# Tile 1's front moved from before the gathers to beside the first 66 slots, and projection passes over tiles 0-1, 2-5, 6-8

## The reference

```python
xn = rms_norm(x, attn_norm)
proj = xn @ w_in                         # 1024 -> 3328: q, k (rotated), v, and 1792 columns for time mixing
o_da = rms_norm(attend(q, k, v, lam), da_subln) * (1.0 - lam_init)      # two softmax maps per head, 4 heads
o_rw = rwkv_time_mix(p_rw, ...)          # recurrent state, 8 heads of 64
h = x + concat([o_da, o_rw]) @ w_out
h = h + peer_ffn(rms_norm(h, ffn_norm), peer_wq, peer_sub_keys, peer_u, peer_v)
```

```python
q = (xb @ wq).reshape(PEER_CHUNK, PEER_HEADS, 2, PEER_KD)
s = jnp.einsum('thcd,hcnd->thcn', q, sub_keys)
sv, si = lax.top_k(s, PEER_TOPK)
cand = (sv[:, :, 0, :, None] + sv[:, :, 1, None, :]).reshape(PEER_CHUNK, PEER_HEADS, -1)
bv, bi = lax.top_k(cand, PEER_TOPK)
act = jax.nn.gelu(jnp.einsum('thkd,td->thk', u_tab[eidx], xb))
return jnp.einsum('thk,thkd->td', gate * act, v_tab[eidx])
```

## Time and profile before

| what | value |
|---|---|
| time, median of 3 runs | 3935.95 us (3930.47 to 3946.15) |
| the profiled execution | 3929.9 us |
| its span, first to last instruction | 3928.1 us |
| busy: PE, DVE, ACT, POOL | 73%, 66%, 33%, 35% of the span |
| moved by DMA | 1431.66 MB, mean 364 GB/s |
| first and last gather issued | 745.5 us, 3895.4 us |

### The profile page before, as it was taken

The page is one execution under the profiler, slowest core; times in us unless marked ns, Lnnn a source line. Parts: engine busy times, 40 slices in busy tenths (PEclk is TensorE's granted clock), DMA queues, the critical chain, the costliest instruction groups (busy, mean ns, idle before and its releaser), DMA issues.

```text
span 3928.1 us, 54696 instructions
## 1 busy us (share of the span) xinstructions
PE 2876.3 (73%) x20366; PEld 1348.2 (34%) x20366; DVE 2599.3 (66%) x5836; ACT 1289.5 (33%) x3597; POOL 1367.6 (35%) x1190
## 2 busy tenths in 40 slices
PE   6899999775678676766766776677576758866565
PEld 3654454342224232322332243224232315521111
DVE  2422456398568948884987598768866776446954
ACT  1311211334332524342434334433433224432232
POOL 1000000244334434443444343434343456533453
PEclk9999999887787787878777777878777667777565
DMA  8534524799999999999999999999999999999998
GB/s 312 196 142 172 194 73 166 307 420 420 422 419 402 420 422 410 419 409 420 413 418 402 419 412 411 385 419 412 393 410 393 375 343 414 405 408 422 416 408 355
DMA packets 254827, 1431.66 MB, mean 364 GB/s; under 512 B 27521, under 2 KB 45457, under 8 KB 110305
## 3 DMA queue, kind: packets, MB, share of 16 engines
q0 software_dynamic: 163232, 1162.26, 72.6%
q1 hardware_dynamic: 91328, 265.89, 17.9%
HBM read 1373.21 MB, written 54.85 MB: 364 GB/s over the span
## 4 chain that ended last, share of the span: by engine, by line
DMA 25%; DVE 17%; PE 16%; issue 5%; POOL 1%; ACT 1%; another core or an unknown queue 0%; SPq 0%; DVEq 0%; ACTq 0%; POOLq 0%
DMA pe_buf<-in_experts,pe_idx 24%; DVE pe_buf L2312 6%; PE pe_psO L1466 4%; PE pe_psH L1448 2%; PE pe_B L1412 2%; POOL pe_buf L1040 1%; PE pe_B L1365 1%; DVE pe_few L2082 1%; PE pe_B L1111 1%; PE pe_B L1304 1%; DMA op_w<-in_w_out 1%; PE pe_B L1395 1%; DVE pe_topi L2191 0%; PE pe_B L1118 0%; PE pe_psW L1436 0%
## 5 line engine op out<-in xcount | busy, mean ns | idle before, releaser
L1040 POOL DMA_INDIRECT pe_buf<-in_experts,pe_idx x1088 | 1281.2, 1178 | 2442.9 <-PE pe_psO L1466 1637.1
L2312 DVE CUSTOM_DVE_ANT_0 pe_buf<-pe_buf,pe_hnR 128x1024 f32<-128x1024 f32 x1088 | 1316.5, 1223 | 695.0 <-DMA pe_buf<-in_experts,pe_idx 647.4
L1466 PE MATMUL pe_psO<-pe_buf,pe_Z 128*32 128x256 f32 x8704 | 843.8, 485 | 631.6 <-ACT pe_Z L1744 599.4
L1738 ACT ACTIVATE pe_gelu<-pe_dot 128x1 f32<-128x1 f32 x1088 | 219.2, 201 | 1622.7 <-DVE pe_dot L2312 1570.2
L1466 PEld LDWEIGHTS pe_psO<-pe_buf,pe_Z 128*32 128x32 f32 x8704 | 215.2, 123 | 1299.0 <-ACT pe_Z L1744 993.5
L1448 PE MATMUL pe_psH<-pe_hn,pe_pick 128*128 128x512 f32 x544 | 415.8, 856 | 44.9 <-ACT pe_hnR L1720 41.3
L1077 PE MATMUL ip_B<-ip_w,ip_xT 128*128 128x512 f32 (+1 forms) x1008 | 430.4, 577 | 16.2 <-DMA ip_w<-in_w_in 16.2
L1744 ACT ACTIVATE pe_Z<-pe_gl,pe_gelu 128x8 f32<-128x8 f32 x1088 | 327.2, 301 | 43.3 <-PE pe_psO L1466 0.4
L1412 PE MATMUL pe_B<-op_wkr,pe_mix 128*128 128x512 f32 (+1 forms) x576 | 270.0, 613 | 9.5 <-DMA op_wkr<-scratch_wk_rows 9.4
L1077 PEld LDWEIGHTS ip_B<-ip_w,ip_xT 128*128 128x128 f32 x1008 | 190.0, 194 | 211.1 <-issue 205.6
L1448 PEld LDWEIGHTS pe_psH<-pe_hn,pe_pick 128*128 128x128 f32 x544 | 108.9, 247 | 175.6 <-issue 88.8
(11 more groups left out here) (344 smaller groups left out, 3600.6 us busy)
## 6 DMA issues: line engine op xcount, KB each, us to landing
op_wkr<-scratch_wk_rows SPq DMA_DIRECT2D x36, 2048.0 KB
ip_w<-in_w_in SPq DMA_DIRECT2D x18, 2048.0 KB, 9.0
op_w<-in_w_out SPq DMA_DIRECT2D x9, 2560.0 KB
pe_buf<-in_experts,pe_idx POOLq DMA_INDIRECT x1088
op_w<-in_w_out SPq DMA_DIRECT2D x9, 1024.0 KB
ip_w<-in_peer_wq SPq DMA_DIRECT2D x4, 2048.0 KB, 11.2
scratch_wk_rows<-wk_wkc SPq DMA_DIRECT2D x16, 512.0 KB, 6.0
tm_ps<-scratch_moved_rows SPq DMA_DIRECT2D x8, 896.0 KB
```

What stands on the lines that cost most here:

```text
L1040: pool.indirect_dma_start(buf[b][:], None, T["experts"], bass.IndirectOffsetOnAxis(ap=idx[:, t % 2, h * NJ + j:h * NJ + j + 1], axis=0)).t ...
L1466: last = nc.tensor.matmul(psO[32 * x:32 * x + 32, j // 4, :], Z[:, n % NZ, 24 - 8 * turn:56 - 8 * turn], buf[home[n]][:, D + x * QUART:D + ...
L1738: nc.scalar.activation(gelu[:, col:col + 1], dot[:, col:col + 1], ACT.Gelu_apprx_tanh).then_inc(f["gelu_done"], 1)
L2312: nc.vector.tensor_tensor_reduce(buf[b][:, 0:D], buf[b][:, 0:D], hnR[:, n // PH % 2, :], 1.0, 0.0, ALU.mult, ALU.add, dot[:, n % (NBUF + E ...
```

## The change

Four things change together.

1. The passes of the projection go over tiles 0-1, 2-5 and 6-8 in place of tile 0, tiles 1-4 and tiles 5-8. The turns move accordingly: four turns stand ahead of the first unit, and four in a row behind the last unit of pass 0. x of tile 1 is loaded ahead of the second block of `w_in`.
2. The front of tile 1 leaves the third phase of the fill, but for its first 20 steps. The other 119 are dealt over slots 0 to 65.
3. The later fronts are dealt with a lag: the front of tile 2 ends at slot 40 of tile 1, that of tile 3 at slot 36 of tile 2, and so on to slot 20 of tile 6 for tile 7. The front of tile 8 ends where it did, at slot 64 of tile 7.
4. `topk` of tile t + 1 can start only when that tile's front has been dealt, so it starts at slot 68 in tile 0 and at slots 42, 38, 34, 30, 26 and 22 in tiles 1 to 6, in place of slot 2. It ends at slot 120 as before.

```diff
-PASSES = ((0,), (1, 2, 3, 4), (5, 6, 7, 8))
+PASSES = ((0, 1), (2, 3, 4, 5), (6, 7, 8))
+N0 = NG * len(PASSES[0])
...
-    steps = [("turn", 0, 0), ("turn", 0, 1)]
+    steps = [("turn", t, half) for t in PASSES[0] for half in range(2)]
...
+NEXT_IN_FILL = 20
...
-        ((("ip", (IP_HALF, IP_STEPS)),), (("tm", 1), ("at", 1), ("op", 1)), (("topk", 0),)))
-DURING = tuple((("tm", t + 2), ("at", t + 2), ("op", t + 2)) for t in range(LAST - 1))
+        ((("ip", (IP_HALF, IP_STEPS)),), (("next", (0, NEXT_IN_FILL)),), (("topk", 0),)))
+NEXT = (("tm", 1), ("at", 1), ("op", 1))
+DURING = ((("next", (NEXT_IN_FILL, None)),),)
+DURING += tuple((("tm", t + 2), ("at", t + 2), ("op", t + 2)) for t in range(LAST - 1))
...
-TOPK_FROM, TOPK_FROM_LAST, TOPK_TO = 2, 66, 120
+LATE = (40, 36, 32, 28, 24, 20) + (LAST_OP_BY,)
+FRONT_BY = (66,) + tuple((t + 1) * 128 + late for t, late in enumerate(LATE))
+TOPK_FROM = (68,) + tuple(late + 2 for late in LATE)
+TOPK_TO = 120
...
-        length = PER if t < len(DURING) - 1 else PER + LAST_OP_BY
+        length = FRONT_BY[t] - len(plan)
...
                         load_w(0)
+                        load_x(1)
+                        load_rope(0)
                         load_w(1)
-                        load_rope(0)
-                        load_x(1)
```

More of the change, by code:

```diff
@@ L12 @@
+import itertools
 from contextlib import ExitStack
@@ L151 @@
 NU = NG * NT
-PASSES = ((0,), (1, 2, 3, 4), (5, 6, 7, 8))
+PASSES = ((0, 1), (2, 3, 4, 5), (6, 7, 8))
+N0 = NG * len(PASSES[0])
 UNITS = tuple((t, n) for tiles in PASSES for n in range(NG) for t in tiles)
 def turns_after(g):
[L159 to L164, removed]
+    after = {(0, 1): [(2, 0)], (1, 1): [(2, 1)], (0, 3): [(3, 0)], (1, 3): [(3, 1)],
+             (1, NG - 1): [(4, 0), (4, 1), (5, 0), (5, 1)], (2, NG - 1): [(6, 0)], (3, NG - 1): [(6, 1), (7, 0)],
+             (4, NG - 1): [(7, 1)], (6, 0): [(8, 0), (8, 1)]}
+    return after.get(UNITS[g], [])
 def fold_order():
@@ L232, in steps_of @@
         return arg[1] - arg[0]
+    if stage == "next":
+        return sum(steps_of(i) for i in NEXT) - arg[0] if arg[1] is None else arg[1] - arg[0]
     if stage == "at":
@@ L244, in costs_of @@
             costs += [ip_cost(i) for i in range(*item[1])]
+        elif item[0] == "next":
+            costs += costs_of(NEXT)[item[1][0]:item[1][1]]
         else:
@@ L324, in topk_pulls @@
     def topk_pulls(t, k):
-        first = TOPK_FROM if t < LAST - 1 else TOPK_FROM_LAST
+        first = TOPK_FROM[t]
         n = TOPK_TO - first
@@ L334, in through @@
             for kind, arg in items:
-                yield from range(arg) if kind == "gap" else stage[kind](arg)
+                if kind == "next":
+                    yield from itertools.islice(following, steps_of((kind, arg)))
+                else:
+                    yield from range(arg) if kind == "gap" else stage[kind](arg)
+        following = through(NEXT)
         for streams in FILL:
@@ L365, in bank_of @@
     def bank_of(g):
-        return (g if g < NG else g + len(FOLD)) % 3
+        return (g if g < N0 else g + len(FOLD)) % 3
     def evicted(eng, units):
@@ L378, in fold_bank @@
     def fold_bank(u):
-        return (NG + u) % 3
+        return (N0 + u) % 3
     def fold_evicted(u):
@@ L1063, in project @@
                             pe.wait_ge(ip["xT"], 2 * t + 2)
-                            if NG <= g < NG + 3:
-                                half, n_ = fold_evicted(len(FOLD) + g - NG - 3)
+                            if N0 <= g < N0 + 3:
+                                half, n_ = fold_evicted(len(FOLD) + g - N0 - 3)
                                 pe.wait_ge(wk_out[half], n_)
@@ L1088, in fold_keys @@
                 if u < 3:
[L1089 removed]
+                    pe.wait_ge(ip["copied"], copied_of(N0 + u - 2))
                 else:
```

2 lines of the change are left out of this document (1 added, 1 removed).

## The result

The changed kernel takes **3981.97 us** (3981.05 to 3984.26, four runs) against 3934.14 us (3930.47 to 3946.15, four runs) for the kernel before: ratio **1.0127**, 95% interval 1.0112 to 1.0141. The forecast was 3928 us, no change to be told, in a range from 3880 to 3982 us. It is slower, by about 48 us, and stands at the upper end of that range. The main part grew by more than 110 us, which the prediction named as a sign that it is wrong. The profiled execution has a span of 3982.5 us, 54.4 more than before.

What follows compares the result with a forecast made beforehand. PE was taken to bound the fill and DMA the main part, with DVE close behind. Terms -92 + 40 + 15 + 15 + 8 + 6 = -8 gave 3928 us on the median, range 3880 to 3982.

Steps and rivals of the forecast that it cites:

- the fill: Before the first gather: PE work and waits leave with tile 1's front; -92 us, from -78 to -105.
- moved transfers: Main part: 16.8 MB of loads moved out of the PE-bound start onto DMA at 420 GB/s; +40 us.
- first 66 slots: Tile 0, slots 0 to 65: 119 front steps packed densely, engine chain may hold up slots; +15 us, 0 to +50.
- tile 2's front: Squeezed into 71 slots from slot 66 on, DVE needing 209 us against DMA's 192; +8 us, 0 to +17.
- `topk` beside `tm` and `at`, tiles 3 to 7: 78 us more DVE work against 79 us of gather waits, nearly balancing; +15 us, 0 to +78.
- tile 8's front: It has 172 slots in place of 192 and part of `topk` beside it; +6 us, 0 to +20.
- the second rival: Slots 42 to about 130 of each tile: DVE becomes the bound beside `tm` and `at`; +64, 4000 us; 21%.
- Its test: Slots 42 to 130 of tiles 1 to 5: DMA share 0.95 or less would prove DVE the bound.
- DVE needed ... 209: 71 slots from slot 66: 215 us before, less 23 for 19 dots, plus 17 of `topk`, makes 209 us.
- the fourth rival: First 66 slots: PE at half clock makes them 253 us against 205, +48 not +15; 3961 us; 3%.
- the third: Start before gathers doesn't shrink as it should; its third phase keeps some 30 us; +22, 3958 us; 4%.
- The first: Main part: slots absorb moved `topk` and tile 1's front at DMA's pace; -52, 3884 us; 35%.

Runs made afterwards that it cites:

- the kernels without it: Kernel before and changed kernel, each with DVE's choice of experts left out for tiles 1 to 8: 3900.59 us and 3853.61 us.
- the lag alone: Kernel before with the changed kernel's dealing of the fronts of tiles 2 to 8 and of `topk`; 4009.19 us, ratio 1.0206.
- `topk` over slots 8 to 91: Kernel before with `topk` of tiles 1 to 7 dealt over slots 8 to 91, not 2 to 119, fronts as before; 3980.97 us, ratio 1.0121.
- the passes alone: Changed kernel with the old fill and old dealing, so only passes, turns and x load are new; 3932.61 us, 0.9995 of before.

## Why the prediction was wrong

**Term by term.** What each came to, the losses by the table of the result:

| term | forecast | measured |
|---|---|---|
| the fill | −92 (−78 to −105) | −108 |
| moved transfers | +40 | +41 |
| first 66 slots | +15 | 0 |
| tile 2's front | +8 (0 to 17) | +40 |
| `topk` beside `tm` and `at`, tiles 3 to 7 | +15 (0 to 78) | +70 |
| tile 8's front | +6 | +10 |
| sum | −8 | +53 (profiled +54.4) |

**The step that failed** is "Bounds 0 and +78. I take a fifth, +15", and the sentence before it, "They balance, but not exactly". The 79 us of waits for gathers and the 78 us of more work do not cancel; the term came to +70. By the table of the five stretches DVE had 67 us more work there. Its waits for gathers gave 46 of their 79 us, so they did serve as slack, but only a good half of them. And its waits for PE did not stay as they were, as both the forecast and the second rival had them: they grew from 48 to 71 us and took half of that gain back. The stretches became 49 us longer. The second rival had the place and the price, though not the balance, since it let the waits for gathers stay: 78 + 17 = 95 us; measured 70 + 40 = 110, partly made up by the first 66 slots. Its test, a share of 0.95 or less, was set too low: 0.97 in the later stretches was enough.

That the choice on DVE is needed for this loss, and that neither the moved matmuls nor their bytes make it alone, is shown by the kernels without it. With it the change costs 48 us and without it the change gives 47: 95 us. The losses say nearly the same, 92: 70 in slots 128-768 and 29 of 40 in slots 66-128, less 7 in tile 8's. It needs neither the moved front nor the passes: the lag alone has 54 us of it.

DVE's load alone is not the whole of it either. `topk` over slots 8 to 91 puts as much work on the same slots and loses 68 us in slots 128-768, where the changed kernel loses 115. It is the load together with the lag that costs, and with the lag DVE waits longer for PE (71 us against 33 in the five stretches). Why the lag lengthens these waits was not tried.

**Tile 2's front** failed in what its count left out. "DVE needed ... 209": it was busy for 205.9 us of the stretch 851 to 1097. But it also waited there for PE, 17.0 and 8.4 us, where the first 246.5 us of the old main part had 214.1 of work and 24.9 of waits for gathers and so at most 7.5 us for all else. At 1.5 steps of `tm` and `at` a slot (107 on 72 slots), most of them with `topk` at its new density, the chain between the engines has waits that it didn't have at 1.2 (107 on 91). Without the choice slots 66-128 still lose 11 us: that part does not need the choice.

**The fill** was undersized, beyond its bound of −105. Forecast were 83 us less of PE's work and 9 less of idle time (−10 − 12 + 13); PE was busy for 585.5 us in place of 675.0, −89.5, and idle for 51.7 in place of 70.5, −18.8. The units' matmuls alone were busy for 9.7 us less (420.7 against 430.4). Of the idle time the start gave 14 us, of which the next window took 6 back, and the third phase gave 9 (12.1 us idle of 192.2 against 21.4 of 300.5). The windows of the first 260 us, changed kernel and kernel before:

```profile
0.00:140.00 140.00, 110.11 (x298) 56.96 (x299) 34.08 (x73) 20.07 (x35) 16.42 (x38) 0.92 0.73 249
140.00:260.00 120.00, 112.42 (x1145) 84.31 (x1145) 54.91 (x91) 32.42 (x60) 0.00 (x0) 0.97 0.51 184
```

```profile
0.00:140.00 140.00, 96.44 (x424) 63.48 (x425) 45.06 (x85) 33.60 (x61) 16.44 (x38) 0.89 0.83 292
140.00:260.00 120.00, 118.53 (x1068) 73.89 (x1067) 45.34 (x84) 16.32 (x29) 0.00 (x0) 1.00 0.37 128
```

PE works 14 us more in the first window and 6 less in the second. Its largest waits are now those of turns for DVE's copy, that for `w_in` has gone from 16.2 us to 6.1:

```profile
PE pe_psW L1071 <- DVE ip_xT L1814: 9.6, 5, 6.0
...
PE ip_B L1091 <- DMA ip_w<-in_w_in: 6.1, 1, 6.1
```

With the passes alone the same 14 us are won at the start, 7 go in the second window, and PE is idle for 27.9 us in the third phase (271.65 busy of 299.5) where it was for 21.4 before: the first gather comes 1 us earlier. With the front moved out the third phase was idle for 12.1 us only, so there they were not lost again.

**The first 66 slots** were right in the sum and too careful in the term: 213.9 us from the first gather to slot 66's dot, at a share of 1.01. With no `topk` on these slots 119 steps of front go at DMA's pace. PE's granted clock over the middle of it, 651 to 851 us, was 0.87 of the full 2.4 GHz:

```profile
651.00:851.00 200.00, 159.16 (x1392) 74.80 (x1388) 111.79 (x219) 77.55 (x214) 74.37 (x67) 0.87 1.01 420
```

So the fourth rival, half clock through these slots, fell, and so did the third: the fill shrank by more than forecast. The first, that the slots absorb all (−52 us), nearly came true without the choice (−47 us).

**Open** are two things: why the lag makes DVE's waits for PE longer, and a smaller part of the loss in slots 128-768. Cut tile by tile, the share of DMA fell from 1.01 or 1.00 to 0.98 or 0.99 there, some 46 us of the 70; the rest is packets that took longer (below), and why they did was not tried. Nor were the waits for PE at the state and at the attention's scores taken away: a kernel in which those steps stand a slot later would tell whether DVE's load or the chain is the better place to mend.

## What to carry over

The waits of the second engine for the bounding one are not slack to be netted in full against work that is moved onto it. Here DVE was busy for 86% and waited for gathers for 5%; such waits gave a good half of themselves, while its waits for a third engine grew. So move work onto the slots where the second engine is idle, here `op` without `tm`, `at` or lag, even if it saves half as much in the fill. To price such a move, leave the suspected work out on the crowded engine in both kernels; the difference of the two differences is what that work has to do with it. Then put the work there alone, without the rest of the change, and compare stretch by stretch: here the totals agreed (+45 and +48 us) and the places did not.
